# First tile's value sums as 64 by 64 diagonals on four quarters of TensorE's array, two slots at a time

## What is computed

```python
def block(xb):                       # 128 tokens at a time
    ...
    experts = jnp.take_along_axis(cand_idx, top_i, axis=-1)
    g = jax.nn.softmax(top_v, axis=-1)
    u_e = u[experts]
    v_e = v[experts]
    a = jax.nn.gelu(jnp.einsum('td,thkd->thk', xb, u_e).astype(jnp.float32), approximate=False)
    return jnp.einsum('thk,thkd->td', (g * a).astype(xb.dtype), v_e)
```

## Time and profile before

| | us |
|---|---|
| median of three runs | 1509.73 |
| the three runs | 1510.27, 1509.73, 1503.19 |
| profiled execution, first to last instruction | 1505.4 |
| first tile's value matmuls (L1084), first and last start | 237.6 and 559.4 |
| PE busy | 1229.6 (82%) |
| DVE busy | 881.8 (59%) |
| ACT busy | 494.3 (33%) |
| POOL busy | 287.5 (19%) |
| bytes moved by the transfers | 510.11 MB |

### The profile page before, as it was taken

The page is one execution under the profiler, slowest core; times in us unless marked ns, Lnnn a source line. Parts: engine busy times, 40 slices in busy tenths (PEclk is TensorE's granted clock), DMA queues, the critical chain, the costliest instruction groups (busy, mean ns, idle before and its releaser), DMA issues.

```text
span 1505.4 us, 19518 instructions
## 1 busy us (share of the span) xinstructions
PE 1229.6 (82%) x7108; PEld 870.5 (58%) x7108; DVE 881.8 (59%) x1781; ACT 494.3 (33%) x1226; POOL 287.5 (19%) x295
## 2 busy tenths in 40 slices
PE   6998899898898777844667456877899998899997
PEld 4887566454453237644653442555688975747775
DVE  0756558767799957579977897654412535501003
ACT  2102434323233334344463661311221343612114
POOL 0102014433334342222321222222000000000000
PEclk9999999999999997978788677999999999999999
DMA  9993239999999999999999989999988674378884
GB/s 362 372 302 137 113 118 427 426 426 427 427 427 426 427 413 382 424 425 418 415 426 388 403 327 419 392 426 423 391 285 300 238 259 161 113 249 291 290 306 177
DMA packets 71706, 510.11 MB, mean 339 GB/s; under 512 B 8112, under 2 KB 8256, under 8 KB 10688
## 3 DMA queue, kind: packets, MB, share of 16 engines
q0 software_dynamic: 40400, 290.02, 46.9%
q1 hardware_dynamic: 30640, 216.78, 37.7%
q10 hardware_dynamic: 576, 2.10, 0.4%
HBM read 507.82 MB, written 1.05 MB: 338 GB/s over the span
## 4 chain that ended last, share of the span: by engine, by line
PE 39%; DMA 25%; DVE 20%; issue 10%; ACT 4%; POOL 1%; SPq 0%; DVEq 0%; ACTq 0%; POOLq 0%
DMA arena<-in_experts,arena 11%; PE bank L1110 9%; DMA ring<-in_weights 9%; PE bank L1120 6%; PE bank L1176 5%; PE bank L1140 4%; DVE arena L1933 3%; DVE arena L2192 3%; PE bank L1084 3%; DMA junk<-in_experts,arena 3%; DMA arena<-in_ada_weights 2%; PE bank L1041 2%; DVE arena L2199 2%; PE bank L968 2%; DVE arena L2211 1%
## 5 line engine op out<-in xcount | busy, mean ns | idle before, releaser
L1110 PE MATMUL bank<-act_t,ring 128*128 128x128 f32 x2048 | 255.0, 287 | 26.5 <-DMA ring<-in_weights 16.9
L1110 PEld LDWEIGHTS bank<-act_t,ring 128*128 128x128 f32 x2048 | 249.3, 202 | 45.9 <-issue 37.6
L1084 PE MATMUL bank<-arena,diag 128*128 128x512 f32 x512 | 239.6, 619 | 41.5 <-ACT diag L1601 41.2
L1084 PEld LDWEIGHTS bank<-arena,diag 128*128 128x128 f32 x512 | 97.0, 197 | 171.4 <-issue 104.3
L2192 DVE SCALAR_TENSOR_TENSOR arena<-arena,bank 128x1024 f32<-128x1024 f32 x128 | 153.8, 1219 | 60.6 <-DMA arena<-in_experts,arena 59.4
L689 POOL DMA_INDIRECT arena<-in_experts,arena x128 | 128.8, 1006 | 285.0 <-PE bank L1084 163.9
L2199 DVE SCALAR_TENSOR_TENSOR arena<-arena,bank 128x1024 f32<-128x1024 f32 x109 | 132.4, 1215 | 80.8 <-DMA arena<-in_experts,arena 80.6
L715 POOL DMA_INDIRECT arena<-in_experts,arena x109 | 112.9, 1036 | 329.0 <-DVE arena L2211 294.0
L1120 PE MATMUL bank<-ring,act_t 128*128 128x256 f32 x704 | 162.0, 390 | 13.2 <-DMA ring<-in_weights 8.2
L1120 PEld LDWEIGHTS bank<-ring,act_t 128*128 128x128 f32 x704 | 136.0, 195 | 37.2 <-issue 6.8
L2211 DVE SCALAR_TENSOR_TENSOR arena<-arena 128x1024 f32<-128x1024 f32 x108 | 138.1, 1279 | 4.1 <-ACT arena L1621 4.0
(11 more groups left out here) (310 smaller groups left out, 1672.9 us busy)
## 6 DMA issues: line engine op xcount, KB each, us to landing
ring<-in_weights SPq DMA_DIRECT2D x200, 1024.0 KB, 6.6
arena<-in_ada_weights POOLq DMA_DIRECT2D x16, 1024.0 KB, 8.3
arena<-in_experts,arena POOLq DMA_INDIRECT x237, 15.5
arena<-in_rpb POOLq DMA_DIRECT2D x4, 512.0 KB, 16.2
arena<-in_weights SPq DMA_DIRECT2D x2, 1024.0 KB, 8.8
row<-in_rows_in ACTq DMA_DIRECT2D x3, 512.0 KB, 3.7
res<-in_x SPq DMA_DIRECT2D x1, 1024.0 KB, 10.8
arena<-in_ctx_in SPq DMA_DIRECT2D x1, 1024.0 KB, 9.2
```

What stands on the lines that cost most here:

```text
L1084: last = mm(bank(j), diag[:, k % 4, :], bufs[k % N_BUF][:, D + half * 512:D + half * 512 + 512], start=(k == 0), stop=(k == SLOTS - 1))
L1110: last = mm(b[:, at + m * P:at + m * P + P], w[:, c, m * P:m * P + P], act_t[:, c, t * P:t * P + P], start=(c == 0), stop=(c == C - 1))
```

## The change

The 128 by 128 diagonal becomes 128 by 64: partitions 0 to 63 hold the first 64 factors on a 64 by 64 diagonal, partitions 64 to 127 the others. The identity it is scaled from is a sum of two parts of the constant, made once by VectorE. For a pair of slots TensorE then does eight matmuls of 64 rows by 64 columns by 512: for each half of the output columns, the upper 64 tokens of both slots and the lower 64 tokens of both. The upper tokens' sums go to one bank and the lower tokens' to another; within a bank, one slot's sum lies on partitions 0 to 63 and the other's on 64 to 127, so that four matmuls in a row use four different quarters of the array. `peer` takes four banks (6, 7, 2, 3), the queries' and keys' jobs of this part go round two banks instead of four, and `gate2` moves to banks 0 and 1 and one group earlier. At the end ScalarE copies the half of each bank that lies on the wrong partitions into SBUF, VectorE adds the other half to it, and gate and residual follow at full width. A pair's two buffers are freed together, and the last pair's two slots are no longer handled apart.

```diff
-GATE2_AFTER, X_NAT1_AFTER = 46, 48
+GATE2_AFTER, X_NAT1_AFTER = 45, 48
...
-        diag = sb("diag", [P, 4, P])
+        diag = sb("diag", [P, 4, DH])
+        ident_half = sb("ident_half", [P, DH])[:, :]
...
-                jobs(("wq", *QUERY_AFTER[g]), 1)
+                jobs(("wq", *QUERY_AFTER[g]), 1, (0, 1))
...
-        jobs(("x_nat", 0), 2, (4, 5)), jobs("peer", 2, (6, 7))
-        jobs("gate2", 2, (2, 3)), jobs(("x_nat", 1), 2, (0, 1))
+        jobs(("x_nat", 0), 2, (4, 5)), jobs("peer", 4, (6, 7, 2, 3))
+        jobs("gate2", 2, (0, 1)), jobs(("x_nat", 1), 2, (0, 1))
...
-            for k in range(SLOTS):
-                pe.wait_ge(diag_ready, k + 1)
-                for half in range(2):
-                    j = JOB["peer"] + half
-                    last = mm(bank(j), diag[:, k % 4, :], bufs[k % N_BUF][:, D + half * 512:D + half * 512 + 512],
-                              start=(k == 0), stop=(k == SLOTS - 1))
...
-                if k < SLOTS - 1:
-                    last.then_inc(freed[k % N_BUF], 1)
...
+            def value_pair(g):
+                first, final = g == 0, g == PAIRS - 1
+                pe.wait_ge(diag_ready, GROUP * g + GROUP)
                 for half in range(2):
+                    for i in range(2):
+                        j, rows = JOB["peer"] + 2 * i + half, slice(i * DH, i * DH + DH)
+                        for s in range(GROUP):
+                            k, lo = GROUP * g + s, (i + s) % 2 * DH
+                            last = mm(bank(j)[lo:lo + DH, :], diag[rows, k % 4, :],
+                                      bufs[k % N_BUF][rows, D + half * 512:D + half * 512 + 512],
+                                      start=first, stop=final, skip_group_check=True)
...
+                            if final and s == GROUP - 1:
+                                last.then_inc(filled[bank_of[j]], 1)
+                            elif not final and half == 1 and i == 1:
+                                last.then_inc(freed[k % N_BUF], 1)
...
+            for k in range(4):
+                is_filled(pe, JOB["peer"] + k)
+            for k in range(SLOTS - GROUP, SLOTS):
+                pe.sem_inc(freed[k % N_BUF], 1)
...
+                        fn(diag[:, k % 4, :], ident_half, ACT.Copy, scale=factors[:, 0, k:k + 1]).then_inc(diag_ready, 1)
...
                     load_root()
+                    for k in range(4):
+                        is_filled(act, JOB["peer"] + k)
+                    for half in range(2):
+                        for i in range(2):
+                            mine, other = slice(i * DH, i * DH + DH), slice(DH - i * DH, 2 * DH - i * DH)
+                            fn(own.hat[mine, half * 512:half * 512 + 512], bank(JOB["peer"] + 2 * i + half)[other, :], ACT.Copy)\
+                                .then_inc(peer_moved, 1)
...
-                    link(v.tensor_tensor(bank(j), bank(j), gate_row2[:, at], ALU.mult))
-                    v.tensor_tensor(res[:, 0, at], res[:, 0, at], bank(j), ALU.add).then_inc(emptied[bank_of[j]], 1)
...
+                        v.tensor_tensor(both[rows, at], bank(j)[rows, :], both[rows, at], ALU.add).then_inc(emptied[bank_of[j]], 1)
...
+                link(v.tensor_tensor(both, both, gate_row2, ALU.mult))
+                v.tensor_tensor(res[:, 0, :], res[:, 0, :], both, ALU.add).then_inc(res_ready, 1)
```

More of the change, by code:

```diff
@@ L366, in build @@
         emptied = [sem(f"bank_emptied{b}") for b in range(8)]
+        ident_half_ready = sem("ident_half_ready")
+        peer_moved = sem("peer_moved")
         silu_zero = sem("silu_zero")
@@ new lines, in _ @@
+            for g in range(PAIRS):
+                value_pair(g)
+                if g in QUERY_AFTER:
+                    tile_query(*QUERY_AFTER[g])
+                if g in KEY_AFTER:
+                    tile_key(*KEY_AFTER[g])
+                if g == GATE2_AFTER:
+                    gate_rows("gate2", 5)
+                if g == X_NAT1_AFTER:
+                    x_nat(1)
+            for k in range(4):
+                is_filled(pe, JOB["peer"] + k)
+            for k in range(SLOTS - GROUP, SLOTS):
+                pe.sem_inc(freed[k % N_BUF], 1)
@@ L1583, in _ @@
             tile_key(3, 0)
+            act.wait_ge(ident_half_ready, 1)
             for g in range(SLOTS // GROUP):
@@ L2009, in add_peer @@
             def add_peer():
+                both = own_of[0].hat
                 for half in range(2):
-                    j, at = JOB["peer"] + half, slice(half * 512, half * 512 + 512)
-                    is_filled(dve, j)
-                    link(v.tensor_tensor(bank(j), bank(j), gate_row2[:, at], ALU.mult))
-                    v.tensor_tensor(res[:, 0, at], res[:, 0, at], bank(j), ALU.add).then_inc(emptied[bank_of[j]], 1)
-                for half in range(2):
-                    is_emptied(dve, JOB["peer"] + half)
-                dve.sem_inc(res_ready, 1)
+                    at = slice(half * 512, half * 512 + 512)
+                    for i in range(2):
+                        j, rows = JOB["peer"] + 2 * i + half, slice(i * DH, i * DH + DH)
+                        dve.wait_ge(peer_moved, 2 * half + i + 1)
+                        v.tensor_tensor(both[rows, at], bank(j)[rows, :], both[rows, at], ALU.add).then_inc(emptied[bank_of[j]], 1)
+                for k in range(4):
+                    is_emptied(dve, JOB["peer"] + k)
+                link(v.tensor_tensor(both, both, gate_row2, ALU.mult))
+                v.tensor_tensor(res[:, 0, :], res[:, 0, :], both, ALU.add).then_inc(res_ready, 1)
+                dve.wait_ge(res_ready, RES_AT["peer", 0])
             dve.wait_ge(cols_loaded, 16)
             dve.wait_ge(silu_ready, 2)
+            dve.wait_ge(c1_loaded, 16)
+            v.tensor_tensor(ident_half, c1[:, 0:DH], c1[:, DH:P], ALU.add).then_inc(ident_half_ready, 1)
             norm(0, res, hat)
```

51 lines of the change are left out of this document (17 added, 34 removed).

## The result

| | us |
|---|---|
| before, median of 15 runs | 1504.78 (1497.79 to 1510.27) |
| changed kernel, median of 15 runs | 1511.44 (1507.74 to 1515.87) |
| ratio, 95% interval | 1.0039 (1.0026 to 1.0053) |
| a second measurement, 10 runs against 33 of before | 1.0034 (1.0018 to 1.0051) |
| profiled execution: time, and first to last instruction | 1508.37, 1506.5 |

The change costs 0.39%, 5.9 us of 1505, with an interval from 3.9 to 8.0. That is "within 0.5%", as forecast, and inside the range. The forecast 1512 lies closer to 1511.44 than it deserves: the kernel before came out 5 us faster here than in the three runs shown earlier, so the loss is 5.9 and not the 2.5 I added. That the two times nearly meet is luck.

What follows compares the result with a forecast made beforehand. The prediction took the gathers' transfers to bound the first tile's expert stage. It summed 0 in the stage, 0 for banks and constant, and +2.5 us at the joint on a median of 1509.73 to 1512 us, range 1504 to 1519.

Steps and rivals of the forecast that it cites:

- The gathers set the beat, the quarters gain nothing: First tile's expert stage: gathers need 4.91 us a pair, so 110 us less TensorE time is worth nothing.
- A pair in 1.75 us and a way out: Value sums on TensorE: four quarter matmuls run together, 1.75 us a pair, plus 0.16 for the last one's way out.
- The open part: Value sums: whether row and column halves overlap both at once; taken as yes, 1.75 us a pair.
- Changes of the array's shape, two banks, `gate2`: Expert stage: shape changes 4 us over 320, two banks under 2 us, both hidden by slack; `gate2` moves nothing else.
- The end of the tile: First tile's end: copies and fold make the residual 3.6 us later, 2 to 2.5 at first norm and eighth gather.
- The delay is carried on: Behind the first tile: everything is later by the joint's 2 to 2.5 us, and nothing makes it good soon.
- the rival in which the joint is absorbed: Behind the joint: later waits of VectorE or TensorE take up the 2.5 us, time 1509.7; chance 20%.
- The signs of being wrong: Profile afterwards: last dot moved over 2 us, a pair over 4.9 us, or a joint delay that has grown.
- The third sign: End of the second tile's gathers: the joint's delay of 2 to 3 us has grown by then.
- +2.5 at the joint: Between the first and second tile: the only nonzero term of the sum, 2.5 us added to the execution time.
- half clock at the end only: Last pair of the first tile: half clock or two quarters at a time, +4.2 us, 1514; chance 20%.
- The clock makes TensorE the bound: Expert stage: idle TensorE drops to half clock and becomes the bound, +8 to +32 us; chance 7%.

Runs made afterwards that it cites:

- no_fold: The changed kernel without ScalarE's four copies; VectorE gates and adds the first two banks as the kernel before did. Ratio to before 1.0003 (0.9986 to 1.0020).
- half_gather: The kernel before and the changed kernel, each with the first tile's gathers bringing 4 KB rows instead of 8. Ratios to before 0.9814 and 0.9701.
- joint_later: The changed kernel with sixteen extra ScalarE copies of 64 x 512 ahead of the fold, read by nobody. Ratio to before 1.0114 (1.0092 to 1.0137).
- copies_twice: The changed kernel with ScalarE's four copies done twice, first into a place nobody reads. Ratio to before 1.0040 (1.0025 to 1.0056).
- joint_shorter: The kernel before with VectorE doing the second tile's first dots in another order at the joint. Ratio to before 1.0002 (0.9988 to 1.0017).
- joint_shorter_quarters: The changed kernel with the fold done one half at a time and VectorE's second-tile dots in another order. Ratio to before 1.0012 (1.0000 to 1.0023).

## Why the prediction was right, and where it was not

- *The gathers set the beat, the quarters gain nothing.* Right. 335.4 us from first gather to last dot in the kernel before and 335.4 (213.4 to 548.8) in the changed one, at 1.01 and 426 GB/s; no_fold cannot be told from before in time, and half_gather shows what the gain is once the cover is gone.
- *A pair in 1.75 us and a way out.* Right where the clock is full: 1.95 us. The open part, both directions at once, has no price that the row shows.
- *Changes of the array's shape, two banks, `gate2`.* No cost shown: no_fold holds them all. Each by itself was not tried.
- *The end of the tile.* Right in mechanism, 0.6 us short in size: 4.2 instead of 3.6 at the residual, 2.9 instead of 2 to 2.5 at the gather. The four copies took 2.44 us as costed. What I had not given is ScalarE's start behind TensorE (0.17 us) and the adds. I had the last add end 0.69 behind the last copy; VectorE starts 0.73 us behind ScalarE, its four adds take 2.85, and the last one ends 1.14 behind the last copy. At the first norm's output I had 2 to 2.5, and 3.7 are measured: one of the two waits that VectorE takes back comes behind it.
- *The delay is carried on.* Right: joint_later shows it with 9.7 us, and the changed kernel's interval (from 3.9 us) puts out the rival in which the joint is absorbed (20%). With 2 us more or less (copies_twice, joint_shorter) no carrying can be told from none.
- *The signs of being wrong.* No pair took 4.9 us, and the last dot kept its distance from the first gather; by itself it lies 6.6 us earlier, so that sign should have been tied to the first gather. The third sign, a delay that has grown by the end of the second tile's gathers, did show: 4.8 and 6.3 us there against 2.9 at the joint, though one kernel's own profiles differ by up to 4. "From there on everything is later by that" was thus too simple, and what adds to the delay on the way is not known.
- *The term that was mis-sized* is the sum's "+2.5 at the joint": measured are 5.9 and 5.1 us, and the profiles give 2.9 at the joint, 4.8 to 6.3 at the second tile's last gather and 3.0 to 4.0 at the end. The rival "half clock at the end only" is not an alternative but happens in some executions: the last pair takes 3.63 us in the profile of joint_shorter_quarters and 1.95 to 1.97 in the other eight with quarters, both of the changed kernel among them, and it adds up to 1.7 us where it happens. How often that is in the timed runs is not known. What adds 2 to 3 us to the 2.9 of the gather stays open. It can lie in the fold, in stages behind the joint, or in the quarters themselves, for which no_fold leaves room up to 3.0 us.
- *The clock makes TensorE the bound.* Right to be kept small: the clock fell (0.50 at 540 us), and the records' busy time fell only by a third; but a pair at half clock, 3.69 us, is still under the beat of 4.9, and the stage did not lengthen. The Trainium skill, "TensorE: Matmul & The Clock Gate", section "HAM oscillation", tells of short bursts between transfer waits that start at half clock, and the trace agrees (0.50 at 540 us). That most of the 110 us would be given back, as I had it by that rule, did not come: it was about 37 of 115.

## What to carry to other kernels

Before an engine is made faster, find what sets the beat of its stage: an engine at 90% that others wait for 164 us is still not the bound if the transfer engines have no idle time. A layout that speeds up the middle and needs a fold at the end pays for the fold where nothing covers it, at the joint between two stages, and there a delay can be carried to the end, as 9.7 us were here; whether one of 2 us is, these runs could not tell. Where single profiles of one kernel differ by more than the effect, compare distances between two events of the program, and leave the total to many timed runs.

## What the runs showed of the hardware that I had not expected

Float32 matmuls of 64 by 64 run four at a time on the four quarters, 1.95 us for sixteen records of 512 columns where the whole array takes 7.13 for sixteen, so 3.6 for eight and the same work. Naming each quarter twice in a row gives the same overlap (1.97 us). With the shorter bursts the granted clock fell (0.98 and 0.93 to 0.86 and 0.75), which took back about 37 us of the 115 that they would have saved at full clock: 161.8 against 125 (64 x 1.95), from 239.6. The clock also makes two executions of the same kernel differ by 3.7 us at one place far behind the change (3.62 and 15.99 us against 1.97 and 13.98).
